# Hybrid decoder layer: the first head's values reloaded in two parts, output weights and residual blocks loaded later

## The chip, the cores and the metric

One Trainium2 chip; the same program runs on 8 of its cores, each on its own 2048 tokens (two sequences of 8192, four cores each), with the 2048 tokens before them as a halo. The metric is the device time of the slowest core in microseconds.

## What is computed

One decoder layer on x (2, 8192, 1024). A parallel mixer, a cross-attention into 256 memory tokens and a SwiGLU network, each behind an RMS norm and added to the residual. The change concerns the attention of the mixer and the loads for what follows it. Cut to that:

```python
proj = rms_norm(x) @ w_in                       # q: 3 groups x 4 heads x 128, k, v: 4 heads x 128, u: 512
for g, (window, dilation) in enumerate(((128, 1), (512, 4), (2048, 16))):
    # query t attends to t - j*dilation, j = 0..window//dilation, shared k and v of head h
    acc[g], m[g], l[g] = dilated_branch(q[:, :, g], k, v, window, dilation)
attn = sum(w[g] * acc[g]) / sum(w[g] * l[g])    # merged over the three groups
h = x + concat([attn, pooled(u)]) @ w_out       # output projection
h = h + cross_attention(rms_norm(h), mem)       # w_cq, w_ckv, w_co
h = h + swiglu(rms_norm(h))                     # d_ff 2816
```

## The kernel before

**Stage 1** walks over 32 tiles of 128 tokens (16 halo, 16 own). For each tile it makes products of the tile of x with the column chunks of w_in (k, v, q0, q1, q2, u). K and Q are kept, transposed, in four slabs of the arena, one per head. V is written tile by tile to a scratch tensor in HBM (`v_scr`, `v_post`), from the ACT queue, since each dilation wants V gathered in another way. Tile 31 comes last, then the u chunks of tiles 28 to 31.

**Attention** has 48 units: `units = (h, r4, g)`, 4 heads, 4 residues of the position modulo 4, and the groups g = 2, 1, 0 (dilation 16, 4, 1). For each unit `S_stage` makes 8, 5 or 17 score matmuls (1024 columns in all) in one of two score tiles in PSUM, ScalarE takes the exponential (128x1024), VectorE multiplies by a mask, and two units later `PV_stage` makes as many numerator matmuls with V and 2 or 3 denominator matmuls with a block of ones. After three units `fin` divides. So three units have 68 matmuls, a head 272.

**V of a head** comes back from HBM in three loads on SP's queue (`load_v`): 1024 KB for dilation 16 (`v16`), 640 KB for dilation 4 (`v4`), 544 KB for dilation 1 (`v1`, runs of 256 bytes). There are two V buffers: V of head h + 2 takes the place of V of head h. The buffer of head 0 lies over the x tiles 20 to 27, that of head 1 over the w_in chunks 2, 3 and 4, of which chunk 2 (u) is read last in stage 1.

**The other loads.** `late_loads`, at unit 1, puts the masks of residues 1 to 3 (768 KB, read as 1.5 MB of float32) on the GpSimd queue, then V of head 1 on SP's, then the output weights `wout` (two loads of 1024 KB) on GpSimd's. The residual blocks xr (2048 KB each, `load_h`) take the place of K and Q slabs that are done with; the memory tokens (`memt`) and the weights w_ckv, w_cq and w_co come at the ends of heads.

**Order.** The program is written once as a list of operations with reads and writes. `order` (line 104) makes each engine's stream of it: it takes, again and again, the operation that can start first by fixed costs, within 160 operations of the oldest open one (40 for a transfer). All transfers go over one modelled bus, so a transfer that is placed early in the program delays the modelled arrival of those behind it, and with it the matmuls that read them. The streams are fixed in the program; on the chip semaphores hold them.

**After attention** `O_units` (output projection of 512 tokens each, added to the residual block), the norms, cross-attention and the feed-forward network are woven together.

Line 306 is every matmul, 309 every transpose, 317 ScalarE's operations, 324, 335 and 339 VectorE's or GpSimd's, 352 a transfer issued by SP, ACT or GpSimd, 355 a load of weights with conversion to bfloat16 on the GpSimd queue.

Of the kernel before, what the change touches and what calls it, by code (L numbers as in the profile page):

```python
# [248 lines left out]
def build_program():  # L249
# [22 lines left out]
    with es:  # L272
# [78 lines left out]
        def DMA(q, out, in_, r, w, **kw):  # L351
            return P.dma(q, lambda e: e.dma_start(out=out, in_=in_, **kw), r, w, nbytes(in_))  # L352
# [36 lines left out]
        def over(keys):  # L389
            return [("~", k) for k in keys]  # L390
# [30 lines left out]
        def load_x(T0, n, r=()):  # L421
            b = T0 // 4
            o = xb[(b + 2) % 3][:, (T0 % 4) * 1024:(T0 % 4 + n) * 1024].rearrange("p (t c) -> p t c", t=n)
            DMA("pool", o, xt_d[T0:T0 + n].rearrange("t p c -> p t c"), list(r),
                [("x", T0 + t) for t in range(n)] + [("~", ("x", T0 + t - 12)) for t in range(n)])
# [215 lines left out]
        for t in range(20, 32):  # L641
# [18 lines left out]
                ("v", 20): [lambda: load_x(24, 4), lambda: WLOAD(mk16, mask_d[:, 0:256], ["mk16"]),  # L660
                            lambda: WLOAD(mk4, mask_d[:, 256:1280], ["mk4"]),
                            lambda: WLOAD(mk1_0, mask_d[:, 1280:2304], [("mk1", 0)])],
                ("v", 24): [lambda: load_x(28, 4)]}
        slot = 0
        seen = set()
        held = {}
        for kind, T in seq:
# [10 lines left out]
            else:  # L678
# [7 lines left out]
                else:  # L686
# [1 line left out]
            run_slot(slot)  # L688
            slot += 1


        VB = [164 * KB, 124 * KB]
        wkeys = lambda cs: [("w", c, kc) for c in cs for kc in range(8)]
        vb_old = [[("x", T) for T in range(20, 28)], wkeys([2, 3, 4])]
        v16 = [view(VB[i], 4096, BF16) for i in range(2)]
        v4 = [view(VB[i] + 8 * KB, 2560, BF16) for i in range(2)]
        v1 = [view(VB[i] + 13 * KB, 17 * 128, BF16) for i in range(2)]
        attnT = view(108 * KB, 4 * 2048, BF16)
        mk1 = [mk1_0] + [view(142 * KB + i * 2 * KB, 1024, BF16) for i in range(3)]
        Pt = [view(156 * KB + i * 2 * KB, 1024, BF16) for i in range(4)]  # L700
        rdt = [view(154 * KB, 512, F32), view(Z + 16 * KB, 512, F32)]
        wout = view(Z, 8192, BF16)
        stage1_small = [("qs", i, j, h) for i in range(3) for j in range(2) for h in range(4)] + [("rt1", i) for i in range(2)] + [("rt2", i) for i in range(2)] + \
                       [("vst", i) for i in range(4)] + [("ust", i) for i in range(3)]

        def load_v(h):
            i = h % 2
            old = [("~", k) for k in vb_old[i]] if h < 2 else []
            vd = v_dram[h]
            allv = [("vd", T) for T in range(32)]  # L710
            DMA("sp", v16[i].rearrange("p (a c) -> p a c", a=2), vd.rearrange("(a p r) d -> p a (r d)", a=2, r=16),
                allv, [("v16", i)] + old)
            DMA("sp", v4[i].rearrange("p (a c) -> p a c", a=5), vd[1536:4096].rearrange("(a p r) d -> p a (r d)", a=5, r=4),
                allv, [("v4", i)] + old)
            DMA("sp", v1[i].rearrange("p (a c) -> p a c", a=17), vd[1920:4096].rearrange("(a p) d -> p a d", a=17),
                allv, [("v1", i)] + old)

        load_v(0)

        def late_loads():  # L720
            WLOAD(view(142 * KB, 3072, BF16), mask_d[:, 2304:5376], [("mk1", i) for i in (1, 2, 3)] + [("~", k) for k in wkeys([4, 5])])
            load_v(1)
            for i in range(2):
                WLOAD(wout[:, i * 4096:(i + 1) * 4096], w_out_d[:, i * 4096:(i + 1) * 4096], [("wout", i)] + [("~", k) for k in stage1_small])

        units = [(h, r4, g) for h in range(4) for r4 in range(4) for g in (2, 1, 0)]
        first_num = set()
# [111 lines left out]
        for u in range(n_u + LAG):  # L839
            run_slot(slot)  # L840
            slot += 1
            if u < n_u:
                S_stage(u)
            v = u - LAG
            if v >= 0:
                PV_stage(v)
                if v % 3 == 2:
                    fin(v // 3)
                h, r4, g = units[v]
                if v == 1:  # L850
                    late_loads()
                if r4 == 3 and g == 0:
                    if h + 2 < 4:
                        load_v(h + 2)
                    if h != 2:
                        load_h(h)
                    if h == 1:
                        DMA("sp", memf, mem_d, (), ["memf"] + over(slabkeys(1)))
                    if h == 2:
                        for i in range(2):  # L860
                            WLOAD(wckv[:, i * 4096:(i + 1) * 4096], w_ckv_d[:, i * 4096:(i + 1) * 4096],
                                  [("wckv", i)] + over(vkeys(0)))
                    if h == 3:
                        WLOAD(wcq, w_cq_d, ["wcq"] + over(slabkeys(3)))
                        WLOAD(wco, w_co_d, ["wco"] + over(slabkeys(3)))
        while pend:
# [242 lines left out]

        weave(O_units(0), (mem_norm_steps(), 0.0, 0.8))  # L1110
        load_h(2)
        weave(O_units(1), (R_steps(0), 0.0, 0.8), (mem_kv_steps(), 0.3, 1.0))
        weave(O_units(2), (R_steps(1), 0.0, 0.8), (Q_steps(0), 0.1, 1.0))
        weave(O_units(3), (R_steps(2), 0.0, 0.8), (X_steps(0), 0.1, 0.9), (Q_steps(1), 0.1, 1.0))
# [216 lines left out]
```

How the kernel before makes its waits and increments, by code:

```python
            def run_stream(e, eh):  # L186
                known = {}
                nw = 0
                for o in self.streams[e]:
                    waits = {}
                    for d in o.deps:
                        key = id(d.sem)
                        if known.get(key, 0) >= d.val:
                            continue
                        if key not in waits or waits[key][1] < d.val:
                            waits[key] = (d.sem, d.val)
                    if o.is_dma and o.prev_val > 0:
                        key = id(o.sem)
                        if known.get(key, 0) < o.prev_val:
                            if key not in waits or waits[key][1] < o.prev_val:
                                waits[key] = (o.sem, o.prev_val)
                    for key, (s, v) in waits.items():
                        eh.wait_ge(s, v)
                        known[key] = v
                        nw += 1
                    ins = o.emit(eh)
                    if o.is_dma:
                        ins.then_inc(o.sem, 16)
                    elif o.needs_inc:
                        ins.then_inc(o.sem, 1)
                if e == "sp":
                    for o in final_wait_ops:
                        if known.get(id(o.sem), 0) < o.val:
                            eh.wait_ge(o.sem, o.val)
                            known[id(o.sem)] = o.val
                stats[e] = (len(self.streams[e]), nw)
```

## Time and profile before

| | us |
|---|---|
| median of 3 runs | 1018.22 (1016.47 to 1074.41) |
| profiled execution, slowest core | 1017.06 |
| its span on core 2, first to last instruction | 1015.5 |
| TensorE busy in it | 957.7 (94%) |
| VectorE, ScalarE, GpSimd busy | 425.3, 385.6, 170.4 |

The page of the profile shows one execution on the slowest core, core 2. The time of the execution is 1.56 us more than this span. Stage 1 ends near 302 us, attention near 390 us; the feed-forward network fills the last half. Busy time of TensorE includes what a slow clock stretches, and a wait is told by its releaser: the semaphore that came last. "issue" is time in which the engine waited for nothing that the profile shows.

### The profile page before, as it was taken

The numbers are of one execution on the slowest core, as the hardware profiler recorded it, in microseconds if no ns is written. First come the engines' busy times: TensorE is split into PE (matmuls) and PEld (weight loads), VectorE is DVE, ScalarE is ACT, GpSimd is POOL, SyncE is SP. The second block draws the span as 40 slices with busy tenths as digits, with TensorE's granted clock in tenths as the row PEclk, the third lists the DMA queues.
The fourth block names the chain that finished last, engine by engine and source line by source line (L and its number), as shares of the span: only waits on it lengthen the run. The fifth ranks groups of instructions, "written<-read, shape, count | busy, mean of one in ns | idle before, by whom it ended". The sixth has DMA issues, their size and how long they took to land.

```text
span 1015.5 us, 16680 instructions; the slowest of 8 cores (1004.2 to 1015.5 us)
## 1 busy us (share of the span) xinstructions
PE 957.7 (94%) x5647; PEld 481.1 (47%) x5752; DVE 425.3 (42%) x934; ACT 385.6 (38%) x726; POOL 170.4 (17%) x253
## 2 busy tenths in 40 slices
PE   2889999999998789999999999999999999999998
PEld 1445545555556675434443444444444444444443
DVE  2436784666764455546677221211133211211111
ACT  3436656555557784446784111111011111111000
POOL 1224452333340011211220000020120000010000
PEclk9989999999998999999999999999999999999999
DMA  9876434110049779300040345547565255538461
GB/s 240 200 126 164 112 53 77 27 38 12 16 107 187 220 211 185 113 0 1 2 84 0 50 76 83 83 76 123 115 115 133 42 83 84 83 60 139 90 133 59
DMA packets 65586, 96.44 MB, mean 95 GB/s; under 512 B 27616, under 2 KB 38752, under 8 KB 63328
## 3 DMA queue, kind: packets, MB, share of 16 engines
q0 software_dynamic: 28496, 50.96, 31.8%
q1 hardware_dynamic: 19968, 40.09, 12.6%
q10 hardware_dynamic: 17040, 4.33, 2.0%
q8 instruction: 48, 0.79, 0.3%
q14 instruction: 34, 0.28, 0.1%
HBM read 133.74 MB, written 12.58 MB: 144 GB/s over the span
## 4 chain that ended last, share of the span: by engine, by line
PE 87%; DMA 4%; issue 2%; ACT 2%; DVE 2%; ACTq 1%; POOL 0%; SPq 0%; DVEq 0%; POOLq 0%
PE psall L306 86%; DMA arena<-v_scr 3%; ACT arena L317 2%; PE psall L309 2%; DMA arena<-xt 1%; DVE arena L335 1%; ACTq L352 1%; DVE arena L324 1%; POOL arena L324 0%; DVE arena L339 0%; DVE arena L329 0%; ACT L317 0%; DVE arena L346 0%; SPq L352 0%; ACTq L203 0%
## 5 line engine op out<-in xcount | busy, mean ns | idle before, releaser
L306 PE MATMUL psall<-arena 128*128 128x512 bf16 (+5 forms) x5327 | 946.0, 335 | 50.9 <-DMA arena<-xt 13.0
L306 PEld LDWEIGHTS psall<-arena 128*128 128x128 bf16 x5432 | 461.0, 100 | 514.4 <-issue 77.6
L317 ACT ACTIVATE arena<-psall 128x512 bf16<-128x512 f32 (+4 forms) x350 | 225.6, 670 | 340.5 <-PE psall L306 316.2
L324 POOL TENSOR_TENSOR arena<-arena 128x256 f32<-128x256 bf16 (+4 forms) x192 | 124.5, 661 | 312.1 <-DVE arena L335 178.0
L324 DVE TENSOR_TENSOR arena<-arena,psall 128x512 bf16<-128x512 f32 x88 | 60.5, 688 | 241.5 <-PE psall L306 232.2
L317 ACT ACTIVATE arena<-arena 128x512 bf16<-128x512 f32 (+6 forms) x292 | 114.2, 410 | 122.2 <-PE psall L306 63.2
L324 DVE TENSOR_TENSOR arena<-psall,arena 128x512 f32<-128x512 f32 (+1 forms) x128 | 86.6, 688 | 172.0 <-PE psall L306 162.5
L335 DVE SCALAR_TENSOR_TENSOR arena<-psall,arena 128x128 bf16<-128x128 f32 (+2 forms) x372 | 111.2, 357 | 61.8 <-ACT arena L317 33.2
L339 DVE TENSOR_REDUCE arena<-arena 128x4 f32<-128x512 bf16 x80 | 54.0, 681 | 50.0 <-ACT arena L317 49.8
L317 ACT ACTIVATE arena<-psall,arena 128x512 bf16<-128x512 f32 (+2 forms) x78 | 52.1, 670 | 39.4 <-PE psall L306 37.3
L355 POOL DMA_DIRECT2D arena<-w_gu_t x22 | 16.6, 753 | 279.1 <-PE psall L306 279.1
L335 DVE SCALAR_TENSOR_TENSOR arena<-arena 128x512 bf16<-128x512 f32 (+2 forms) x75 | 53.5, 750 | 9.5 <-ACT arena L317 8.9
L324 DVE TENSOR_TENSOR arena<-arena 128x1024 bf16<-128x1024 bf16 (+2 forms) x50 | 34.6, 694 | 35.0 <-ACT arena L317 30.2
L309 PEld LDWEIGHTS psall<-arena 128*128 128x128 bf16 x320 | 22.0, 98 | 15.6 <-issue 4.3
L309 PE MATMUL psall<-arena 128*128 128x128 bf16 x320 | 26.5, 219 | 3.1 <-POOL arena L324 3.1
L346 DVE COPY arena<-psall 128x512 bf16<-128x512 bf16 x48 | 24.3, 506 | 11.8 <-PE psall L306 9.7
L317 ACT ACT_TABLE_LOAD x6 | 7.7, 1283 | 47.0 <-PE psall L306 30.2
L355 POOL DMA_DIRECT2D arena<-w_d_t x8 | 7.2, 898 | 108.6 <-PE psall L306 108.6
L355 POOL DMA_DIRECT2D arena<-w_ckv_t x2 | 1.5, 744 | 62.4 <-PE psall L306 62.4
L352 POOL DMA_DIRECT2D arena<-xt x11 | 8.2, 746 | 21.6 <-DMA arena<-xt 19.1
L329 DVE TENSOR_SCALAR arena<-arena 128x512 bf16<-128x512 f32 (+3 forms) x23 | 11.3, 519 | 0.1
L329 POOL TENSOR_SCALAR arena<-arena 128x512 bf16<-128x512 f32 x4 | 6.2, 1561 | 0.0
(14 smaller groups left out, 15.8 us busy)
## 6 DMA issues: line engine op xcount, KB each, us to landing
arena<-w_gu_t POOLq DMA_DIRECT2D x22, 1024.0 KB, 8.6
arena<-w_in_t SPq DMA_DIRECT2D x12, 1024.0 KB, 7.6
arena<-w_d_t POOLq DMA_DIRECT2D x8, 1408.0 KB, 17.5
arena<-xr SPq DMA_DIRECT2D x4, 2048.0 KB, 12.3
outT<-arena SPq DMA_DIRECT2D x32, 256.0 KB, 3.6
arena<-xt POOLq DMA_DIRECT2D x7, 1024.0 KB, 12.3
v_scr<-arena ACTq DMA_DIRECT2D x32, 128.0 KB, 2.7
arena<-v_scr SPq DMA_DIRECT2D x4, 1024.0 KB, 8.1
```

The costliest lines, as they stand in the source:

```text
L306: P.op("pe", lambda e: e.matmul(out, lhsT=lhsT, rhs=rhs, start=start, stop=stop), r, w, max(0.056, 0.003 + size(out) / 2400))
L309: P.op("pe", lambda e: e.transpose(out=out, in_=in_, identity=ident), r, w, 0.057)
L317: P.op("act", lambda e: e.activation(out=out, in_=in_, func=func, **kw), r, w, 0.18 + 0.00085 * size(out))
L324: P.op(eng, lambda e: e.tensor_tensor(out=out, in0=in0, in1=in1, op=op), r, w, dcost(eng, size(out), per))
L329: P.op(eng, lambda e: e.tensor_scalar(out=out, in0=in0, scalar1=s1, scalar2=None, op0=op0), r, w, c)
L335: P.op("dve", lambda e: e.scalar_tensor_tensor(out=out, in0=in0, scalar=scalar, in1=in1, op0=op0, op1=op1, **kw), r, w, dcost("dve", size( ...
L339: P.op("dve", lambda e: e.tensor_reduce(out=out, in_=in_, axis=mybir.AxisListType.X, op=ALU.add), r, w, dcost("dve", size(in_), 0.00105))
L346: P.op(eng, lambda e: e.tensor_copy(out=out, in_=in_), r, w, dcost(eng, size(out), 0.0009))
L352: return P.dma(q, lambda e: e.dma_start(out=out, in_=in_, **kw), r, w, nbytes(in_))
L355: return P.dma("pool", lambda e: e.dma_start(out=out, in_=in_, max_dma_last_dim=4096), r, w, nbytes(in_))
```

## The change

Three things are done.

1. V of head 0 is loaded in two parts. Part 0 is issued at tile 29 of stage 1 and waits for the writes of V of tiles 0 to 27 only: the first half of `v16`, 96 of 128 partitions of its second half, 4 of 5 blocks of `v4`, 13 of 17 of `v1`. Part 1, at the old place, loads the rest (128 KB each) and waits for part 0 and all writes. Heads 1 to 3 are loaded as before.
2. The output weights move from unit 1 to unit 12 (`wout_loads`), and they read the key of the last V load of head 1, so their issue waits until it has landed.
3. The residual blocks 0 and 1 were loaded at the ends of heads 0 and 1; they are now loaded at the ends of heads 2 and 3. Block 3 moves from the end of head 3 to behind block 2, after the first piece of the projection.

```diff
@@ todo of stage 1
-                ("v", 24): [lambda: load_x(28, 4)]}
+                ("v", 24): [lambda: load_x(28, 4)], ("v", 29): [lambda: load_v(0, 0)]}
...
+        def load_v(h, part=None):
+            i = h % 2
+            old = over(vb_old[i]) if h < 2 else []
+            vd = v_dram[h]
+            dep = {0: range(28), 1: range(28, 32), None: range(32)}[part]
+            allv = [("vd", T) for T in dep]
...
+            elif part == 0:
+                DMA("sp", o16[:, 0:1, :], s16[:, 0:1, :], allv, [("v16a", i)] + old)
+                DMA("sp", o16[0:96, 1:2, :], s16[0:96, 1:2, :], allv, [("v16b", i)] + old)
+                DMA("sp", o4[:, 0:4, :], s4[:, 0:4, :], allv, [("v4a", i)] + old)
+                DMA("sp", o1[:, 0:13, :], s1[:, 0:13, :], allv, [("v1a", i)] + old)
+            else:
+                DMA("sp", o16[96:128, 1:2, :], s16[96:128, 1:2, :], allv + [("v16a", i), ("v16b", i)], [("v16", i)] + old)
+                DMA("sp", o4[:, 4:5, :], s4[:, 4:5, :], allv + [("v4a", i)], [("v4", i)] + old)
+                DMA("sp", o1[:, 13:17, :], s1[:, 13:17, :], allv + [("v1a", i)], [("v1", i)] + old)
...
-        load_v(0)
+        load_v(0, 1)
 
         def late_loads():
             WLOAD(view(142 * KB, 3072, BF16), mask_d[:, 2304:5376], [("mk1", i) for i in (1, 2, 3)] + [("~", k) for k in wkeys([4, 5])])
             load_v(1)
+
+        def wout_loads():
             for i in range(2):
-                WLOAD(wout[:, i * 4096:(i + 1) * 4096], w_out_d[:, i * 4096:(i + 1) * 4096], [("wout", i)] + [("~", k) for k in stage1_small])
+                WLOAD(wout[:, i * 4096:(i + 1) * 4096], w_out_d[:, i * 4096:(i + 1) * 4096], [("wout", i)] + over(stage1_small),
+                      r=[("v1", 1)])
@@ the loop over the units
                 if v == 1:
                     late_loads()
+                if v == 12:
+                    wout_loads()
                 if r4 == 3 and g == 0:
                     if h + 2 < 4:
                         load_v(h + 2)
-                    if h != 2:
-                        load_h(h)
                     if h == 1:
                         DMA("sp", memf, mem_d, (), ["memf"] + over(slabkeys(1)))
                     if h == 2:
+                        load_h(0)
...
                     if h == 3:
+                        load_h(1)
                         WLOAD(wcq, w_cq_d, ["wcq"] + over(slabkeys(3)))
...
         weave(O_units(0), (mem_norm_steps(), 0.0, 0.8))
         load_h(2)
+        load_h(3)
```

The stream of SP from the last w_in chunks on, before (`v_scr` rows are V loads: 128x2x2048 is dilation 16, 128x5x512 dilation 4, 128x17x128 dilation 1; xr is a residual block):

```order
L352 DMA arena<-w_in_t 128x2048 x4
L352 DMA arena<-v_scr 128x2x2048
L352 DMA arena<-v_scr 128x5x512
L352 DMA arena<-v_scr 128x17x128
L352 DMA arena<-v_scr 128x2x2048
L352 DMA arena<-v_scr 128x5x512
L352 DMA arena<-v_scr 128x17x128
L352 DMA arena<-v_scr 128x2x2048
L352 DMA arena<-v_scr 128x5x512
L352 DMA arena<-xr 128x4096
L352 DMA arena<-v_scr 128x17x128
```

The same place of SP now, up to the last V load of head 1:

```order
L352 DMA arena<-w_in_t 128x2048 x4
L352 DMA arena<-v_scr 128x2048
L352 DMA arena<-v_scr 96x2048
L352 DMA arena<-v_scr 128x4x512
L352 DMA arena<-v_scr 128x13x128
L352 DMA arena<-v_scr 32x2048
L352 DMA arena<-v_scr 128x512
L352 DMA arena<-v_scr 128x4x128
L352 DMA arena<-v_scr 128x2x2048
L352 DMA arena<-v_scr 128x5x512
L352 DMA arena<-v_scr 128x17x128
```

Seven smaller loads of head 0 stand for three. The residual block that stood inside V of head 2 is gone from there; all four blocks now follow the last V load of head 3.

The stream of TensorE in head 2 before, from the denominators of its first three units on (128x4x16 x15 with 128x4x8 x2 are the seventeen numerators of dilation 1, 128x8x4x16 to 128x2x4x8 its denominators, 128x64 x15 with 128x32 x2 its scores, 128x128 x8 scores or numerators of dilation 16):

```order
L306 MATMUL psall<-arena 128x8x4x16
L306 MATMUL psall<-arena 128x7x4x16
L306 MATMUL psall<-arena 128x2x4x8
L306 MATMUL psall<-arena 128x128 x8
L306 MATMUL psall<-arena 128x4x16 x15
L306 MATMUL psall<-arena 128x4x8 x2
L306 MATMUL psall<-arena 128x4x16 x15
L306 MATMUL psall<-arena 128x4x8 x2
L306 MATMUL psall<-arena 128x64 x15
L306 MATMUL psall<-arena 128x32 x2
L306 MATMUL psall<-arena 128x64 x4
```

And now, in the same head:

```order
L306 MATMUL psall<-arena 128x4x16 x15
L306 MATMUL psall<-arena 128x4x8 x2
L306 MATMUL psall<-arena 128x8x4x16
L306 MATMUL psall<-arena 128x7x4x16
L306 MATMUL psall<-arena 128x2x4x8
L306 MATMUL psall<-arena 128x64 x15
L306 MATMUL psall<-arena 128x32 x2
L306 MATMUL psall<-arena 128x128 x8
```

Before, the numerators of two units of dilation 1 stood in one run, behind the denominators of both; the same happened in head 3. Now each unit's numerators stand ahead of its denominators throughout head 2, and in head 3 the numerators of one unit alone come late, between two denominator matmuls of the unit behind it. The stream of GpSimd is the same row for row: the output weights were and are its next transfers behind the masks, and only what they wait for is new.

## Rows read from the trace of the kernel before

**Rows 1.** Cores: span and mean granted TensorE clock.
```profile
core 1: 1012.5 us, clock 0.997
core 2: 1015.5 us, clock 0.992
...
core 4: 1004.2 us, clock 0.998
...
core 6: 1013.9 us, clock 0.993
```

**Rows 2.** Chain that ended last, core 2: start us, length us, what.
```profile
302.13 32.95 DMA arena<-v_scr
```

**Rows 3.** Timeline of TensorE, core 2: start us, length us, group [idle before <-releaser].
```profile
305.62 8.42 PE L306 MATMUL psall<-arena 128*128 128x64 bf16 x130 [0.51 <-ACT arena L317]
317.38 11.00 PE L306 MATMUL psall<-arena 128*128 128x64 bf16 x134 [3.34 <-DVE arena L324]
328.53 4.25 PE L306 MATMUL psall<-arena 128*128 128x64 bf16 x67 [0.15 <-DVE arena L324]
335.33 5.44 PE L306 MATMUL psall<-arena 128*128 128x64 bf16 x87 [2.55 <-DMA arena<-v_scr]
343.32 8.99 PE L306 MATMUL psall<-arena 128*128 128x64 bf16 x114 [2.56 <-issue]
```

**Rows 4.** Waits, core 2, 295 to 400 us: total us, times, longest us.
```profile
DVE arena L324 <- DMA arena<-masks: 4.5, 1, 4.5
...
PE psall L306 <- issue: 2.6, 1, 2.6
PE psall L306 <- DMA arena<-v_scr: 2.5, 1, 2.5
```

**Rows 5.** Windows, core 2: length, busy (x), then PEclk, DMA share, GB/s.
```profile
315.00:320.00 5.00, 2.62 (x39) 2.15 (x40) 2.49 (x4) 0.81 (x2) 0.00 (x0) 0.64 1.05 175
320.00:325.00 5.00, 4.95 (x52) 3.97 (x51) 2.08 (x3) 3.13 (x4) 0.00 (x0) 0.68 1.05 167
...
340.00:345.00 5.00, 2.44 (x41) 2.02 (x38) 1.83 (x3) 2.73 (x4) 0.00 (x0) 0.87 0.82 254
345.00:350.00 5.00, 4.95 (x68) 4.10 (x68) 1.88 (x3) 2.82 (x5) 0.00 (x0) 0.79 0.14 36
```

**Rows 6.** DMA, core 2, 302 to 320 us; issues with KB and us to landing.
```profile
q0 software_dynamic: 732, 1.47, 54.5%
q1 hardware_dynamic: 1170, 1.76, 39.8%
...
arena<-v_scr SPq DMA_DIRECT2D x1, 544.0 KB, 33.0
```

**Rows 7.** DMA, core 2, the V loads of head 0: issue, then us to landing.
```profile
288.78 1.47 SPq L352 DMA_DIRECT2D arena<-v_scr  x3
...
arena<-v_scr SPq DMA_DIRECT2D x1, 544.0 KB, 10.5
```

**Rows 8.** Timeline of GpSimd, core 2: issue of the output weights.
```profile
309.32 1.52 POOL L355 DMA_DIRECT2D arena<-w_out_t  x2 [7.59 <-PE psall L306]
```

**Rows 9.** Windows, core 4: length, busy (matmuls first), PEclk, DMA share, GB/s.
```profile
315.40:344.60 29.20, 26.11 (x410) 21.63 (x417) 16.60 (x24) 24.52 (x31) 0.00 (x0) 1.00 0.87 219
344.80:373.50 28.70, 24.42 (x390) 20.32 (x396) 16.31 (x24) 23.92 (x31) 3.20 (x4) 1.00 0.89 242
```

**Rows 10.** Timeline of TensorE, core 4.
```profile
333.67 2.46 PE L306 MATMUL psall<-arena 128*128 128x64 bf16 x40 [2.24 <-issue]
```

**Rows 11.** Timeline of SP's queue, core 2.
```profile
328.57 2.48 SPq L352 DMA_DIRECT2D arena<-xr  x1
331.57 20.32 SPq L352 DMA_DIRECT2D arena<-v_scr  x3
...
388.72 18.03 SPq L352 DMA_DIRECT2D arena<-xr  x2
```

**Rows 12.** Waits of TensorE, 295 to 420 us: core 1, then core 6.
```profile
PE psall L306 <- DMA arena<-v_scr: 1.0, 1, 1.0
...
PE psall L306 <- DMA arena<-v_scr: 3.1, 1, 3.1
```

More of the change, by code:

```diff
@@ L662, in build_program @@
                             lambda: WLOAD(mk1_0, mask_d[:, 1280:2304], [("mk1", 0)])],
-                ("v", 24): [lambda: load_x(28, 4)]}
+                ("v", 24): [lambda: load_x(28, 4)], ("v", 29): [lambda: load_v(0, 0)]}
+        VB = [164 * KB, 124 * KB]
+        wkeys = lambda cs: [("w", c, kc) for c in cs for kc in range(8)]
+        vb_old = [[("x", T) for T in range(20, 28)], wkeys([2, 3, 4])]
+        v16 = [view(VB[i], 4096, BF16) for i in range(2)]
+        v4 = [view(VB[i] + 8 * KB, 2560, BF16) for i in range(2)]
@@ new lines, in build_program @@
+        v1 = [view(VB[i] + 13 * KB, 17 * 128, BF16) for i in range(2)]
+        attnT = view(108 * KB, 4 * 2048, BF16)
+        mk1 = [mk1_0] + [view(142 * KB + i * 2 * KB, 1024, BF16) for i in range(3)]
+        Pt = [view(156 * KB + i * 2 * KB, 1024, BF16) for i in range(4)]
+        rdt = [view(154 * KB, 512, F32), view(Z + 16 * KB, 512, F32)]
+        wout = view(Z, 8192, BF16)
+        stage1_small = [("qs", i, j, h) for i in range(3) for j in range(2) for h in range(4)] + [("rt1", i) for i in range(2)] + [("rt2", i) for i in range(2)] + \
+                       [("vst", i) for i in range(4)] + [("ust", i) for i in range(3)]
@@ new lines, in load_v @@
+        def load_v(h, part=None):
[4 more added lines that the diff above has]
+            allv = [("vd", T) for T in dep]
+            o16 = v16[i].rearrange("p (a c) -> p a c", a=2)
+            s16 = vd.rearrange("(a p r) d -> p a (r d)", a=2, r=16)
+            o4, s4 = v4[i].rearrange("p (a c) -> p a c", a=5), vd[1536:4096].rearrange("(a p r) d -> p a (r d)", a=5, r=4)
+            o1, s1 = v1[i].rearrange("p (a c) -> p a c", a=17), vd[1920:4096].rearrange("(a p) d -> p a d", a=17)
+            if part is None:
+                DMA("sp", o16, s16, allv, [("v16", i)] + old)
+                DMA("sp", o4, s4, allv, [("v4", i)] + old)
+                DMA("sp", o1, s1, allv, [("v1", i)] + old)
+            elif part == 0:
[7 more added lines that the diff above has]
+                DMA("sp", o1[:, 13:17, :], s1[:, 13:17, :], allv + [("v1a", i)], [("v1", i)] + old)
@@ L689, in build_program @@
             slot += 1
[L692 to L716, printed above, removed]
-        load_v(0)
+        load_v(0, 1)
         def late_loads():
```

## The prediction

> **What bounds the kernel now.** I read the spans of the cores first [rows 1]. The job ends with its slowest core: core 2 needs 1015.5 us, core 4, which does the same work, 1004.2 us. So some 11 us of core 2's span are waits, not work. Then the chain that ended last: it is TensorE nearly throughout, and its longest piece that isn't is a transfer of the values V into the arena, from 302 to 335 us [rows 2]. That is where attention begins. The timeline of TensorE there [rows 3] shows three stops on core 2: 3.34 us before 317.38, 2.55 us before 335.33, 2.56 us before 343.32. The waits of that stretch [rows 4] name the first two. VectorE waited for the masks (4.5 us) and TensorE for VectorE; then TensorE waited for V. The third has no releaser, only "issue". The windows [rows 5] show what a stop costs on top: after the first the granted clock is 0.64 and 0.68 for 10 us, after the last 0.87 and 0.79 (a mix of full 2.4 GHz and 1.2 GHz).
>
> The reader is to see who fills the DMA engines in that stretch. From 302 to 320 us the GpSimd queue (masks, then output weights) takes 54.5% of the sixteen engines, SP's queue (V of head 1) 39.8%; together they are full. The last V transfer of head 1, 544 KB, takes 33.0 us to land [rows 6]. The same 544 KB of head 0, with no such company, took 10.5 us [rows 7].
>
> **The split load of head 0.** Before, its three loads are issued from 288.78 us on and have landed by about 300.4 [rows 7]. TensorE comes to the first products with V only in the stretch that begins at 305.62 us, and the one wait for V in these waits is the later one of 2.55 us [rows 3, 4]. So there is nothing to gain on this path: 0. It adds four DMA issues on SP, which has nothing else to do then, some 1.9 MB of reading while the last four tiles of stage 1 run, and 0.4 MB behind the last write of V. I count 0 to 1 us of cost. The Trainium skill (DMA: Bandwidth & Descriptors, Rules for kernel authors) says of two transfers to disjoint partition halves that they serialise and aren't worth it. By that rule this part is a small loss of fixed costs; the row gives it no wait to shorten either, so both leave the sum as it is.
>
> **The output weights, off the path of V of head 1.** They were issued at 309.32 us [rows 8]; now they wait until the last V load of head 1 has landed. In rows 6 the GpSimd queue spends 54.5% of 18 us, 9.8 us of all engines, on 1.47 MB, or 6.7 us per MB; SP's spends 7.2 us on 1.76 MB, or 4.1 us per MB. Masks (0.79 MB) then cost 5.2 us, V of a head (2.26 MB) 9.3 us, the weights (2.1 MB) 14 us. The transfers start near 303.4 us, so masks and V of head 1 are done by 318, say 320 with the landing. TensorE wants the last of them at 328.53 + 4.25 = 332.8 us [rows 3]. The wait of 2.55 us goes. The next thing late there is VectorE or ScalarE by a few tenths. With it goes most of the half-speed window: 0.13 and 0.21 of 5 us each are 1.7 us of lost clock [rows 5]; I take 1.5, bounds 0 and 1.7.
>
> **The order of heads 2 and 3.** The stream of each engine comes from a list scheduler that charges every transfer to one bus. With the early residual block and weights gone, it moves matmuls: before, in heads 2 and 3, the seventeen numerators of two groups stood in a row and three score tiles bunched behind them; now the pattern of heads 0 and 1 goes on through head 2, and in head 3 one group is displaced by a little. What the bunching costs stands in the windows of core 4 [rows 9]. From 315.40 to 344.60 us 410 matmuls take 29.20 us with one stop of 2.24 [rows 10], so 26.96 / 410 = 65.8 ns each; from 344.80 to 373.50 us 390 take 28.70, or 73.6 ns, with no stop like it. A head has 272, so two heads lose 2 x 272 x 7.8 ns = 4.2 us. Since a piece of disorder stays in head 3, I take 4.0, bounds 0 and 4.2. This is paid on every core.
>
> **The residual blocks.** The block of 2 MB issued at 328.57 us among V of head 2, and the next one, now stand behind all V loads [rows 11]. They are needed when the projection begins, about 389 us, where the last two blocks are released by the end of the last scores; from 350 us on they have over 30 us. Two blocks of 2.1 MB at 4.1 us per MB take 17 us of all engines. Cover: heads 2 and 3. Cost 0; the queue of SP has nothing behind them that is due.
>
> **The stop marked "issue".** Its length differs by core: 2.56 us on core 2, 2.24 on core 4 [rows 3, 10]. Since no semaphore releases it, I read it as code that comes late because the DMA engines are full. They are full in after too, but without the big residual block. I take 1.5 us left, so 1.0 gained; bounds 2.6 gained and 2.6 lost (a second one in the new full stretch). The Trainium skill (Runtime: NRT & Kernel Launch, Instruction fetch mechanics) calls the cost of crossing a block of instructions mostly hidden. By it this term would be 0; the trace disagrees if my reading of the stop is right.
>
> **What stays.** The masks keep their place and their trigger, so I leave the stop of 3.34 us and its slow window.
>
> Sum for core 2: 2.55 + 1.5 + 4.0 + 1.0 = 9.05, so 1015.5 - 9.05 = 1006.4 us. Core 1 (1012.5 us, V wait 1.0 us [rows 12]) gives 1012.5 - 1.0 - 4.0 - 1.0 = 1006.5; core 6 (1013.9 us, V wait 3.1) gives 1013.9 - 3.1 - 1.5 - 4.0 = 1005.3. The slowest of eight is a little above such estimates: 1007. The profiled execution took 1017.06 us, 1.56 us more than its span, hence 1008.6 us. That execution lies 1.2 us below the median of 1018.22, so a median for the changed kernel is near 1009; I forecast 1009.0.
>
> **Rivals.** (1) The weights starve V of head 2: slower. They now run from about 320 us, and V of head 2 is issued in the ten microseconds after, its last part by 331.57 us [rows 11]. The regular order also wants its last part much sooner: one head after 332.8, that is 332.8 + 272 x 65.8 ns = 350.7 us. By my bus count all is done by 320 + 14 + 9.3 = 343 to 345 us. But if the 544 KB need 33.0 us again, as beside the weights in rows 6, they land at 364.6, TensorE stops for 14 us, and a slow window costs 2 us more (between the 1.7 and 3.4 of rows 5): 1008.6 + 16 = 1024.6 us. It decides from a landing time of 350.7 - 331.6 = 19 us on. For it: that row. Against it: those 33 us also held the masks and the residual block, and the weights here have a lead of some 6 us. The Trainium skill (DMA: Bandwidth & Descriptors, Queues, rings and completion order) has each engine take turns between the queues packet by packet; a late V load would then lose half its rate to the weights for as long as they last, which is the mechanism of this rival, and in rows 6 the two queues do share about evenly.
> (2) The gain is smaller: the stop marked "issue" comes back elsewhere and a longer one is added, and the regular order gives half since ScalarE is nearly full anyway. 1015.5 - 2.55 - 1.5 - 2.0 + 2.6 = 1012.0, so 1013.6 us. For it: the DMA engines stay full from 303 to past 345 us.
> (3) The masks land sooner too, because the weights of neighbouring cores no longer run: core 2 gains 3.34 us and up to 3.4 us of clock more [rows 5], but then core 1 sets the end at about 1006, so 1007 us at most and 1004 if "issue" stops shrink too. Against it: the masks are issued before the weights, in the same queue.
>
> **How the numbers follow.** Forecast 0.55, (1) 0.12, (2) 0.23, (3) 0.10. The range for 8 in 10 goes from (3) to beyond (2): 1003 to 1018 us. Faster or slower by over 2% (about what a measurement of this kernel can tell from no change) means below 998 or above 1038.6 us; no case reaches either, which leaves 0.03 and 0.02 for the unforeseen.
>
> **What would show it.** Right: no wait of TensorE for V; the 544 KB of head 1 landed by about 320 us; core 4 at 66 ns per matmul in the stretch of heads 2 and 3; the stop for the masks still there on core 2. Wrong: a stop before the last numerators of head 2's first group (rival 1), new "issue" stops past 340 us (rival 2), masks landing within 12 us on core 2 (rival 3), or a later end of stage 1, moved by the early reads of V.

## The result and the profile after

| | before | after |
|---|---|---|
| median of 5 runs, us | 1018.22 (1016.47 to 1074.41) | 1028.7 (1026.89 to 1157.35) |
| profiled execution | 1017.06 | 1028.79 |
| its span | 1015.5 (core 2) | 1026.9 (core 0) |
| first residual addition of the output projection to the end | 622.2 | 641.4 |

The ratio is 1.0104, 95% interval 1.0086 to 1.0121: slower, by 10.5 us, where 9 us less were forecast. In some executions the cores of one die ran at a lower clock throughout: the medians of this table count them, while the ratio and every time given below leave them out.

In the two profiled executions every core is slower (core 5 by 3.1 us, core 4 by 19.0), so this is in the program, not in one core's luck. The windows of core 0 tell where (length, then busy time and count of TensorE's matmuls, its weight loads, VectorE, ScalarE and GpSimd; then PEclk, DMA share, GB/s):

```profile
300.00:395.00 95.00, 83.81 (x1190) 64.70 (x1205) 50.46 (x75) 74.30 (x100) 12.03 (x16) 1.00 0.91 212
395.00:430.00 35.00, 29.94 (x146) 14.54 (x147) 16.97 (x28) 10.61 (x22) 5.56 (x5) 0.95 0.38 96
430.00:465.00 35.00, 25.76 (x90) 9.54 (x90) 11.67 (x18) 10.93 (x17) 3.12 (x3) 0.76 0.00 0
465.00:1027.00 562.00, 553.85 (x2515) 249.95 (x2565) 162.74 (x239) 130.03 (x208) 46.33 (x52) 1.00 0.43 77
```

The two middle stretches on core 2 of before, begun 7.8 us later since its first residual addition is at 393.29 us and that of after at 385.50:

```profile
402.80:437.80 35.00, 33.96 (x171) 16.31 (x173) 17.64 (x29) 13.64 (x27) 6.45 (x6) 1.00 0.38 97
437.80:472.80 35.00, 33.55 (x150) 14.20 (x152) 20.02 (x30) 18.78 (x30) 6.60 (x6) 1.00 0.00 1
```

From 430 to 465 us TensorE does 90 matmuls where it did 150, its granted clock is 0.76, and no DMA engine is busy. So it isn't a transfer that is waited for. Attention, ahead of it, runs at full clock and better than before. The waits of TensorE show both. First 300 to 395 us of after, core 0 (total us, times, longest), which answers to rows 4 and 12:

```profile
PE psall L306 <- issue: 3.3, 3, 1.9
PE psall L306 <- ACT arena L317: 3.1, 5, 1.2
PE psall L306 <- DVE arena L324: 3.1, 4, 2.5
```

No wait for V is left, on any core. Now 395 to 470 us of after:

```profile
PE psall L306 <- DVE arena L335: 9.0, 5, 3.2
PE psall L306 <- ACT arena L317: 2.6, 4, 1.1
PE psall L306 <- DVE arena L324: 2.4, 1, 2.4
PE psall L306 <- issue: 0.2, 1, 0.2
```

and 387 to 465 us of before, core 2:

```profile
PE psall L306 <- ACT arena L317: 1.3, 4, 0.5
PE psall L306 <- DVE arena L335: 0.8, 1, 0.8
```

That is 14.2 us of stops in place of 2.1. The timeline of TensorE and then of VectorE there (start us, length us, group, [idle before <-releaser]) tells what VectorE was doing:

```profile
439.25 0.38 PE L306 MATMUL psall<-arena 128*128 128x512 bf16 x1 [0.41 <-ACT arena L317]
442.84 2.72 PE L306 MATMUL psall<-arena 128*128 128x512 bf16 x6 [3.21 <-DVE arena L335]
...
447.25 0.58 PE L306 MATMUL psall<-arena 128*128 128x512 bf16 x1 [0.84 <-ACT arena L317]
450.45 3.57 PE L306 MATMUL psall<-arena 128*128 128x512 bf16 x8 [2.62 <-DVE arena L335]
```

```profile
437.30 4.73 DVE L335 SCALAR_TENSOR_TENSOR arena<-arena 128x512 bf16<-128x512 f32 x7 [0.92 <-ACT arena L317]
441.94 0.75 DVE L335 SCALAR_TENSOR_TENSOR arena<-psall,arena 128x512 bf16<-128x512 f32 x1
...
449.55 0.75 DVE L335 SCALAR_TENSOR_TENSOR arena<-psall,arena 128x512 bf16<-128x512 f32 x1 [6.20 <-ACT arena L317]
```

Two kinds of work share line 335, and the operands tell them apart: `arena<-arena` scales a token block by its norm (`rms_steps`), `arena<-psall,arena` scales a query of cross-attention out of PSUM (`norm_tail`), which TensorE's next product reads. Seven of the first kind stand in a row, 4.73 us, and the one for which TensorE waits stands behind them; TensorE has nothing else in its stream at that point and stops for 3.21 us. Later VectorE itself is idle for 6.20 us behind ScalarE, while TensorE runs single matmuls between stops.

VectorE was no quicker at that place in before. Its rows and TensorE's there, core 2:

```profile
438.32 2.74 DVE L335 SCALAR_TENSOR_TENSOR arena<-arena 128x512 bf16<-128x512 f32 x4 [0.92 <-ACT arena L317]
...
442.84 0.75 DVE L335 SCALAR_TENSOR_TENSOR arena<-psall,arena 128x512 bf16<-128x512 f32 x1
```

```profile
441.19 8.34 PE L306 MATMUL psall<-arena 128*128 128x512 bf16 x37 [0.54 <-ACT arena L317]
```

From the start of the row of scalings to the scaling of the query it is 4.52 us in before and 4.64 us after. The difference is that TensorE then ran 37 matmuls in one piece across that scaling, where it now has a single one (at 439.25) and stops. So these rows put the loss in cover that TensorE's stream has lost, not in more work on VectorE. Behind the stops the granted clock is lower: where it was 1.00 it is now 0.95 and 0.76.

The sizes agree: 12.1 us more of stops, and by an estimate from the windows 29.94 x 0.05 + 25.76 x 0.24 = 7.7 us of the busy time lost to the clock, together 19.8 us; the table above has 641.4 - 622.2 = 19.2 us. The end of stage 1 moved little: the group of 25 matmuls that follows its last transposes starts at 304.30 us, before at 303.41. Attention gave its part: from there to the first residual addition it is 81.2 us, before 89.9. The time is lost behind that point and nowhere else.

### The profile page after: what moved, and what is told of

Same layout as the page of the kernel before. It is cut to its first block, busy times and chain, and to the rows that moved or that the text cites. A ratio compares the mean times of both kernels' runs of the same rounds, so it can differ in the third digit from the quotient of the medians.

```text
span 1026.9 us, 16716 instructions; the slowest of 8 cores (1015.6 to 1026.9 us)
## 1 busy us (share of the span) xinstructions
PE 960.3 (94%) x5647; PEld 479.9 (47%) x5752; DVE 425.8 (41%) x934; ACT 385.6 (38%) x726; POOL 170.1 (17%) x253
## 4 chain that ended last, share of the span: by engine, by line
PE 86%; DVE 4%; issue 3%; DMA 3%; ACT 2%; ACTq 1%; POOL 0%; DVEq 0%; POOLq 0%
PE psall L306 85%; ACT arena L317 2%; DVE arena L335 2%; DMA arena<-masks 1%; PE psall L309 1%; DMA arena<-xt 1%; DVE arena L324 1%; ACTq L352 1%; DVE arena L339 1%; DVE arena L329 0%; POOL arena L324 0%; DVE arena L346 0%; ACT L317 0%; DVEq L203 0%; ACTq L203 0%
## 5 line engine op out<-in xcount | busy, mean ns | idle before, releaser
L306 PE MATMUL psall<-arena 128*128 128x512 bf16 (+4 forms) x5327 | 948.5, 335 | 59.6 <-DVE arena L335 15.9
L306 PEld LDWEIGHTS psall<-arena 128*128 128x128 bf16 x5432 | 459.6, 100 | 526.9 <-issue 91.4
L317 ACT ACTIVATE arena<-psall 128x512 bf16<-128x512 f32 (+4 forms) x350 | 226.1, 670 | 333.9 <-PE psall L306 310.6
L324 POOL TENSOR_TENSOR arena<-arena 128x256 f32<-128x256 bf16 (+4 forms) x192 | 124.3, 661 | 331.1 <-DVE arena L335 168.2
L317 ACT ACTIVATE arena<-arena 128x512 bf16<-128x512 f32 (+5 forms) x292 | 113.4, 409 | 137.2 <-PE psall L306 66.8
L324 DVE TENSOR_TENSOR arena<-arena,psall 128x512 bf16<-128x512 f32 x88 | 60.6, 688 | 241.4 <-PE psall L306 235.2
L324 DVE TENSOR_TENSOR arena<-psall,arena 128x512 f32<-128x512 f32 (+1 forms) x128 | 86.7, 688 | 172.7 <-PE psall L306 166.6
L335 DVE SCALAR_TENSOR_TENSOR arena<-psall,arena 128x128 bf16<-128x128 f32 (+2 forms) x372 | 111.2, 357 | 83.8 <-ACT arena L317 48.6
L339 DVE TENSOR_REDUCE arena<-arena 128x4 f32<-128x512 bf16 x80 | 54.0, 681 | 49.2 <-ACT arena L317 49.1
L317 ACT ACTIVATE arena<-psall,arena 128x512 bf16<-128x512 f32 (+2 forms) x78 | 52.1, 671 | 41.4 <-PE psall L306 38.6
L335 DVE SCALAR_TENSOR_TENSOR arena<-arena 128x512 bf16<-128x512 f32 (+2 forms) x75 | 53.0, 747 | 7.4 <-ACT arena L317 6.9
L324 DVE TENSOR_TENSOR arena<-arena 128x1024 bf16<-128x1024 bf16 (+2 forms) x50 | 34.6, 694 | 25.9 <-ACT arena L317 22.2
L309 PEld LDWEIGHTS psall<-arena 128*128 128x128 bf16 x320 | 22.2, 98 | 15.8 <-issue 4.5
L346 DVE COPY arena<-psall 128x512 bf16<-128x512 bf16 x48 | 24.3, 505 | 12.0 <-PE psall L306 9.7
(14 smaller groups left out, 15.8 us busy)
```

Of the source, the lines that this page charges most:

```text
L306: P.op("pe", lambda e: e.matmul(out, lhsT=lhsT, rhs=rhs, start=start, stop=stop), r, w, max(0.056, 0.003 + size(out) / 2400))
L309: P.op("pe", lambda e: e.transpose(out=out, in_=in_, identity=ident), r, w, 0.057)
L317: P.op("act", lambda e: e.activation(out=out, in_=in_, func=func, **kw), r, w, 0.18 + 0.00085 * size(out))
L324: P.op(eng, lambda e: e.tensor_tensor(out=out, in0=in0, in1=in1, op=op), r, w, dcost(eng, size(out), per))
L335: P.op("dve", lambda e: e.scalar_tensor_tensor(out=out, in0=in0, scalar=scalar, in1=in1, op0=op0, op1=op1, **kw), r, w, dcost("dve", size( ...
L339: P.op("dve", lambda e: e.tensor_reduce(out=out, in_=in_, axis=mybir.AxisListType.X, op=ALU.add), r, w, dcost("dve", size(in_), 0.00105))
```

## Experiments

Three theories. **O**: the loss is the order of the streams behind attention, which the scheduler makes otherwise because the residual blocks now stand on its one modelled bus ahead of the later weights. **T**: the transfers themselves, late or crowded. **S**: the split loads cost in stage 1. The order of TensorE's, ScalarE's and VectorE's computing instructions was read from the built programs, which is why the expectations can speak of it. Before was run beside every kernel; its medians were 1016.83 us (beside e1 to e4), 1016.66 (e5 to e8) and 1017.30 (e9 to e12). The ratio is an estimate of its own from the same executions, so it can differ by 0.001 from the quotient of two medians.

### The first four: parts alone, and order against transfers

**e1**, the residual blocks back:

```diff
                 if h + 2 < 4:
                     load_v(h + 2)
+                if h != 2:
+                    load_h(h)
...
-                    load_h(0)
...
-                    load_h(1)
...
         load_h(2)
-        load_h(3)
```

> The changed kernel with the residual blocks loaded where they were before (blocks 0, 1 and 3 behind the loads of V at the ends of heads 0, 1 and 3), the split V and the late output weights kept. The order of every engine's instructions behind attention is then that of the kernel before. Theory O (the loss is the order of the engines' instructions behind attention, which the residual blocks' new place has changed): the stretch from the first output projection to the end goes back from 646 to about 627 us, the gains at the start of attention stay; 1008 to 1012 us. Theory T (late arrivals or crowding by the late output weights): 1018 us or more. Theory S (the split loads cost in stage 1): 1018 us or more, with stage 1 longer.

Measured 1015.78 us, ratio 0.9987 (0.9974 to 1.0). The loss is gone, as O has it: on core 7 it is 622.3 us from the first residual addition (390.59) to the end. The gain is nearly gone too, which O did not say, so the time misses the 1008 to 1012 us expected. The waits of core 7, 300 to 400 us, show why:

```profile
PE psall L306 <- ACT arena L317: 5.8, 9, 1.2
PE psall L306 <- DMA arena<-v_scr: 3.4, 1, 3.4
```

ScalarE's many short stops are those of before, since the old place of the blocks brings a bunched order of heads 2 and 3 with it; and there is a wait for V again, now at 351 us for head 2, whose last load stands behind residual block 0 on SP's queue and beside the output weights. It is the place that the first rival named, but that rival blamed the weights alone and had 16 us; here it is 3.4 us, and e12 will show that it takes the block.

**e2**, of the whole change the split alone:

```diff
         def late_loads():
...
             load_v(1)
-
-        def wout_loads():
             for i in range(2):
...
-                if v == 12:
-                    wout_loads()
```

(together with e1's diff; the output weights are loaded at unit 1 again and wait for no load of V)

> The kernel before with the split V of head 0 alone; output weights and residual blocks where they were. Theory O: no order of an engine's computing instructions changes, only SP's; the wait for V (2.55 us and a part of the 1.5 us of clock) may go or may stay, as the output weights still stand before it: 1014 to 1018.5 us. Theory S: 1020 us or more.

Measured 1017.01 us, ratio 0.9993 (0.9977 to 1.0008). S is out. The split by itself does nothing that these executions can tell from no change.

**e3**, the changed kernel with before's order behind attention. A table names, for each engine, the stretches of its stream and the operations in them by their number in the program; transfers stay where they are:

```diff
+FIXED = {
+    "pe": [(2992, [(4271, 3), (4267, 1), (4274, 5), (4280, 12),
...
+}
...
+        comp = [o for o in self.ops if not o.is_dma]
+        for e, parts in FIXED.items():
+            st = self.streams[e]
+            at = [i for i, o in enumerate(st) if not o.is_dma]
+            for first, runs in parts:
+                new = [comp[k] for a, n in runs for k in range(a, a + n)]
...
+                for j, o in enumerate(new):
+                    st[at[first + j]] = o
```

> All transfers as in the changed kernel, but a table puts the instructions of TensorE, ScalarE and VectorE behind attention in the order that they have in the kernel before. Theory O: the 18 us of the stretch behind attention come back, 1008 to 1012 us, TensorE's stops of 2 to 3.5 us between 404 and 455 us gone and its clock at 1.00 there. Theory T (the transfers themselves, the residual blocks or weights that land late): 1025 to 1030 us, since every transfer is issued as in the changed kernel.

Of four executions two count, 1009.87 and 1011.57 us (median 1010.72), too few for a ratio. The 18 us are back, with every transfer issued as in the changed kernel: T is out. Windows and waits of the profiled execution, core 5 (the table makes the file longer, so each line has a number higher by 15: L321 is L306, L332 is L317, L339 is L324 and L350 is L335); the waits are those of 387 to 470 us:

```profile
387.00:430.00 43.00, 42.16 (x213) 20.14 (x212) 22.35 (x36) 15.91 (x31) 8.52 (x8) 1.00 0.46 112
430.00:465.00 35.00, 33.59 (x152) 14.05 (x151) 20.32 (x30) 18.60 (x30) 6.70 (x6) 1.00 0.00 1
```

```profile
PE psall L321 <- ACT arena L332: 1.4, 4, 0.5
PE psall L321 <- DVE arena L350: 0.8, 1, 0.8
PE psall L321 <- DVE arena L339: 0.2, 1, 0.2
```

The clock is 1.00 throughout; 2.4 us of stops stand where 14.2 stood. From the first residual addition (385.00 us) to the end of the span (1008.3) it is 623.3 us, where before has 622.2.

**e4**, the converse: the same table code in the kernel before, with the changed kernel's order behind attention.

> All transfers as in the kernel before, but TensorE, ScalarE and VectorE have the changed kernel's order behind attention. Theory O: the loss without the gains, 18 us more than before, 1033 to 1038 us. Theory T: 1016 to 1020 us, as before.

Measured 1035.01 us, ratio 1.0168 (1.0144 to 1.0191), 17 to 18 us over before. The waits of core 2, 390 to 470 us, are those of the changed kernel within 0.3 us, the window shows the clock, and from the first residual addition (392.88) to the end it is 640.9 us:

```profile
PE psall L321 <- DVE arena L350: 9.0, 5, 3.2
PE psall L321 <- DVE arena L339: 2.4, 1, 2.4
PE psall L321 <- ACT arena L332: 2.3, 4, 0.8
```

```profile
430.00:465.00 35.00, 26.06 (x94) 9.97 (x95) 11.45 (x17) 12.12 (x19) 3.12 (x3) 0.83 0.00 1
```

O stands on both legs: the order alone makes the loss, and without it the loss isn't there.

### The next four: what the gain consists of, and a remedy

**e5**, as e3, but the table holds before's order for attention as well.

> All transfers as in the changed kernel, but every engine's computing instructions in the order of the kernel before, in attention too. It differs from e3 only in the order of heads 2 and 3. By the prediction's sum that order is worth 4.0 us of the 7 or so that e3 gained (ScalarE's ten short stops of TensorE, 5.6 us in all, come back for 1.9): 1012 to 1015 us. If the transfers alone made the gain: 1008 to 1011 us. If the order made all of it: 1016 to 1018 us.

Measured 1012.27 us, ratio 0.9947 (0.9929 to 0.9965), as the prediction's sum would have it. So the new transfers alone give 4.4 us by the medians (1016.66 - 1012.27) and 5.4 by the ratio, whose interval allows 3.6 to 7.2. The order of heads 2 and 3 gives some 1.5 on top of it (1012.27 to 1010.72), but with two executions of e3 that can't be told from nothing.

**e6**, the remedy that O suggests. The scheduler's model takes the residual blocks at no cost; on the chip they are transferred as in the changed kernel:

```diff
         def DMA(q, out, in_, r, w, **kw):
-            return P.dma(q, lambda e: e.dma_start(out=out, in_=in_, **kw), r, w, nbytes(in_))
+            return P.dma(q, lambda e: e.dma_start(out=out, in_=in_, **kw), r, w, 0 if w and w[0][0] == "hT" else nbytes(in_))
```

> The changed kernel in which the scheduler's model of the one bus takes the four residual blocks at no cost; nothing else is edited. Attention's order stays the changed kernel's; behind attention the order becomes neither kernel's, nearer that of before. Theory O with the cause in the modelled bus: the loss goes, 1007 to 1013 us. If another order than that of before is as bad as the changed kernel's: 1020 us or more.

Measured 1005.81 us, ratio 0.9884 (0.9841 to 0.9927): with one edit of the model the changed kernel is 23 us faster than it was, and 11 us faster than before by the medians (12 by the ratio). Its four executions (1004.79 to 1008.2 us) also lie under e3's two, so before's order behind attention wasn't the best either. Waits of core 1, 387 to 470 us:

```profile
PE psall L306 <- ACT arena L317: 0.3, 1, 0.3
PE psall L306 <- DVE arena L335: 0.2, 1, 0.2
PE psall L306 <- DVE arena L324: 0.2, 1, 0.2
```

0.7 us of stops, where before had 2.1 and after 14.2. From the first residual addition (384.95) to the end (1005.0) it is 620.1 us, 2.1 under before; the other 8.3 us of the gain lie ahead of it.

**e7**, e6 with the masks in three transfers:

```diff
-            WLOAD(view(142 * KB, 3072, BF16), mask_d[:, 2304:5376], [("mk1", i) for i in (1, 2, 3)] + [("~", k) for k in wkeys([4, 5])])
+            for i in (1, 2, 3):
+                WLOAD(mk1[i], mask_d[:, 1280 + 1024 * i:2304 + 1024 * i], [("mk1", i)] + [("~", k) for k in wkeys([4, 5])])
```

> As e6, and the masks of the late tiles loaded in three transfers of 256 KB in place of one of 768 KB. The stop of TensorE for the masks (2 to 3.3 us on some cores) goes or shrinks: 1 to 4 us under e6. Rival: the two issues more on POOL and the other transfers put back by them cost as much, within 1 us of e6.

Measured 1008.65 us, ratio 0.9906 (0.9869 to 0.9943): 2.8 us over e6 by the medians, outside both expectations. The stop did go: TensorE's longest wait for VectorE between 300 and 387 us is 0.6 us over all eight cores, where e6 has 3.1. But the stops marked "issue" rose from 2.5 to 3.7 us a core (table below). The intervals overlap, so whether it is slower than e6 stays open; a gain of 1 us or more isn't seen.

**e8**, e3 with `load_v(0)` whole again, behind the last tile:

```diff
-                ("v", 24): [lambda: load_x(28, 4)], ("v", 29): [lambda: load_v(0, 0)]}
+                ("v", 24): [lambda: load_x(28, 4)]}
...
-        load_v(0, 1)
+        load_v(0)
```

> As e3, with the values of the first head loaded in one part again, behind the last tile: what the split is worth where the output weights are out of the way. If the split hides the wait: 2 to 4 us more than e3, 1011 to 1014 us, with TensorE waiting 1 to 3 us for V at about 302. If the late output weights alone took that wait away: as e3, 1009 to 1011 us.

Measured 1009.43 us, ratio 0.992 (0.9889 to 0.9951), and no wait for V on any core. The split is worth nothing that can be seen; the late output weights took the wait away.

### The last four: the remedy taken apart

**e9**, the kernel before with the table for attention alone, so that heads 2 and 3 run in the changed kernel's order.

> All transfers as in the kernel before, and behind attention its order too; heads 2 and 3 alone in the changed kernel's order. e3 against e5 gives this order 2 us with the changed kernel's transfers. If it is worth as much with the transfers of before: 1014 to 1016.5 us, ScalarE's ten stops at four. If its gain needs V and the weights in the new order: 1016.5 to 1019 us.

Measured 1014.86 us, ratio 0.9977 (0.9964 to 0.999), 2.4 us under before. Its timeline of TensorE on core 3 shows what takes a part of the gain away:

```profile
336.96 13.21 PE L321 MATMUL psall<-arena 128*128 128x64 bf16 x181 [5.49 <-DMA arena<-v_scr]
```

A wait for V of 5.49 us, where before's cores had 3.1 at most: without the later weights the same load is late.

**e10**, e6's edit in the kernel before, nothing else.

> The kernel before with one edit: the model takes the residual blocks at no cost. Every transfer is issued where it was before; the order behind attention becomes that of e6, and that of attention all but the changed kernel's. If e6's 1005.8 us rests on the order alone: 1005 to 1009 us. If order and transfers each give their part (2 to 5 us for the order of both stretches, 5.7 us for the transfers by e5): 1011 to 1015 us.

Measured 1012.47 us, ratio 0.995 (0.9933 to 0.9968): 4.8 us by orders alone (5.1 by the ratio). Order and transfers each give a part.

**e11**, e6 and e8's diff together: the values in one part, the blocks free in the model.

> As e6, with the values of the first head in one part behind the last tile. e8 against e3 says that the split gives nothing once the output weights are out of the way: 1004 to 1007.5 us. If e3's 1010 us hid a gain of the split: 1008 us or more.

Measured 1007.54 us, ratio 0.9902 (0.9879 to 0.9924). At the expected bound; it is 1.7 us over e6 by the medians, but the intervals overlap.

**e12**, e11 with e1's diff: residual blocks at their old places.

> As e11, with the residual blocks loaded where they were before (ends of heads 0, 1 and 3): block 0 of 2 MB goes ahead of head 2's values, beside the output weights. The order of the computing instructions is that of e6 and e11. If e1's wait for V at 351 us (3.4 us) comes from that block: the wait shows again, 1009 to 1013 us. If the place of the residual blocks doesn't matter to the transfers: 1004 to 1007.5 us.

Measured 1008.80 us, ratio 0.9911 (0.9887 to 0.9935). TensorE on core 7 waits for V of head 2, and the load that it waits for took 24.3 us, where the changed kernel's two loads of that size on core 0 in its stretch from 320 to 350 us took 15.0 in the median:

```profile
353.52 17.32 PE L306 MATMUL psall<-arena 128*128 128x64 bf16 x272 [2.48 <-DMA arena<-v_scr]
```

```profile
arena<-v_scr SPq DMA_DIRECT2D x1, 544.0 KB, 24.3
```

```profile
arena<-v_scr SPq DMA_DIRECT2D x2, 544.0 KB, 15.0
```

The wait that was expected is there, and e11, which has the same weights but not the block at that place, has it on no core. It reaches three of eight cores and costs 1.3 us of the median, within the noise of the two intervals.

All kernels side by side: stops of TensorE between 300 and 387 us, mean over the eight cores of one execution, worked out from the waits of each core (longest single one in brackets); clock as the mean of the cores' windows.

| | V | ScalarE | VectorE | issue | clock 300-387 | clock 387-465 | us |
|---|---|---|---|---|---|---|---|
| before | 1.4 (3.1) | 5.5 | 1.7 (3.3) | 3.4 (3.1) | 0.972 | 0.998 | 1017.3 |
| after | 0 | 1.9 | 1.4 (2.5) | 3.3 (2.4) | 0.990 | 0.883 | 1028.4 |
| e1 | 1.1 (3.4) | 5.5 | 1.1 (2.0) | 2.7 (2.8) | 0.990 | 1.000 | 1015.8 |
| e2 | 0.8 (3.3) | 5.5 | 1.5 (3.1) | 6.0 (8.4) | 0.960 | 1.000 | 1017.0 |
| e3 | 0 | 1.9 | 1.2 (2.5) | 3.1 (2.3) | 0.995 | 1.000 | 1010.7 |
| e4 | 1.6 (4.5) | 5.6 | 1.6 (3.0) | 1.9 (3.1) | 0.985 | 0.895 | 1035.0 |
| e5 | 0 | 5.4 | 0.5 (1.3) | 3.0 (2.8) | 0.995 | 1.000 | 1012.3 |
| e6 | 0 | 1.6 | 1.4 (3.1) | 2.5 (2.3) | 0.992 | 1.000 | 1005.8 |
| e7 | 0.1 (0.5) | 1.8 | 1.1 (0.6) | 3.7 (2.1) | 0.998 | 1.000 | 1008.7 |
| e8 | 0 | 1.9 | 1.0 (1.2) | 3.9 (2.8) | 0.988 | 1.000 | 1009.4 |
| e9 | 2.9 (5.5) | 1.9 | 1.7 (3.2) | 2.2 (2.8) | 0.972 | 1.000 | 1014.9 |
| e10 | 0.3 (1.5) | 1.9 | 2.2 (3.7) | 7.3 (8.8) | 0.953 | 1.000 | 1012.5 |
| e11 | 0 | 2.0 | 1.1 (2.0) | 3.9 (2.8) | 0.990 | 1.000 | 1007.5 |
| e12 | 0.7 (2.5) | 1.9 | 1.8 (2.7) | 3.1 (2.8) | 0.990 | 1.000 | 1008.8 |

(Before's 1017.3 is its median beside e9 to e12.)

## Why the prediction was wrong

The direction was wrong, and one step made it so. The term by term account, in the prediction's own order:

- **Split load, cost 0.** Right as far as the noise allows: e2 has 0.9993, and e8 and e11, without it, can't be told from e3 and e6, which have it.
- **Output weights, 2.55 + 1.5 us.** Right in mechanism, near in size. No core waits for V; the last V load of head 1 lands in 15.8 us after its issue in place of 33.0 [rows 6]; the clock of the stretch rose from 0.972 to 0.990, 1.6 us of 87 (a mean over cores). The weights, which wait for that load, are issued at 320.48 us on core 0, so V had landed by about 320 us, as the sign asked. e5, which holds the orders fixed, gives all transfers together 5.4 us by its ratio where the terms 2.55, 1.5 and 1.0 make 5.05. The load that lands in after, in the DMA view of 302 to 320 us:

```profile
arena<-v_scr SPq DMA_DIRECT2D x1, 544.0 KB, 15.8
```

- **Order of heads 2 and 3, 4.0 us.** The work per matmul fell as said. Core 4 of after, which answers to rows 9, has one unbroken group:

```profile
336.74 37.57 PE L306 MATMUL psall<-arena 128*128 128x64 bf16 x587 [0.63 <-issue]
```

  37.57 / 587 = 64.0 ns, where 65.8 was expected and before had 73.6. ScalarE's stops fell by 3.6 us a core (5.5 to 1.9). Of the time of the kernel it made less: 2.4 us in e9, where the wait for V grew, and about 1.5 from e5 to e3. So 4.0 was about twice too much.
- **"issue", 1.0 us gained.** Wrong: 3.3 us a core against 3.4, and 3.9 in e8 and e11.
- **Masks stay, with their slow window.** Half right. The stop is there on some cores (2.51 us on core 0 of after, 2.38 on core 4) but gone on core 2, which the sign named: there the masks land in 11.2 us in place of 15.5, the sign of rival 3. Cores 0, 4 and 6 still need 14.6 to 14.8 us, and in before cores 4 and 7 had 11.3 already, so rival 3 as a whole did not occur; which core is late changes, and a sign tied to one core says little. The slow window doesn't always follow: the clock from 315 to 320 us is 1.00 on core 0 of after, 0.66 on core 4.
- **Residual blocks, "Cost 0; the queue of SP has nothing behind them that is due".** This is the step that failed. It priced the blocks as transfers on the chip, where they do cost nothing that can be seen (T is out). But they are also entries on the scheduler's modelled bus. The prediction knew that bus and used it for heads 2 and 3, and stopped looking there. At the ends of heads 2 and 3 stand the weights for cross-attention; each block of 2.1 MB ahead of them takes 10 us of a bus modelled at 210 KB per us, so the model thinks the weights late and orders everything behind attention for that. The cost in place of 0 was 17 to 18 us (e4, and e3 against after): e4 shows it without the moved transfers, e6 takes it away with the modelled price of the blocks alone. e6 frees all four blocks at once, so which of them does it isn't shown.
- **Rival 1**, V of head 2 starved by the weights, did not occur: no core of after waits for V. e1 and e12 show a wait at that place, of 3.4 and 2.5 us at most, where block 0 stands ahead of the last of those loads. So moving the blocks helped the queue, by about 1 us, and hurt in the model.
- **The last step of the sum.** 1008.6 us and the 1.2 us by which that execution lay under the median make 1009.8; the text rounds this down to 1009.0. It changes nothing here.

The attention's part of the forecast came out near in size: 7.8 us earlier at the first residual addition, 8.7 from the end of stage 1 on, against 9.05 forecast. In part that is luck. From 300 to 387 us the stops of TensorE fall by 5.0 us between core 2 of before and core 0 of after (14.5 to 9.5), and the clock goes from 0.94 to 1.00, by an estimate 4.3 us of 71.43 busy ones, where the sum has 1.5; that makes up for the order's missing half and for "issue". What was missing is a look at all places at which the new streams differ from the old. The comparison of orders would have shown that TensorE's, ScalarE's and VectorE's streams differ in a second stretch, behind attention, where the trace of before has only 2.1 us of stops, so that a new order could gain about as much (e6 and e10 did) and could lose far more. What is not settled: which of the moved operations there does the harm: the stream of one engine can't be exchanged without the others, since they would wait for each other in a circle, and smaller exchanges weren't tried.

## What to carry to other kernels

Where a scheduler works from modelled costs, a moved transfer is priced twice: on the chip, and in the model, where it can reorder engines far behind the place of the edit. List every stretch in which the streams differ and ask of each how much the trace of before leaves to gain there; one with 2 us of stops can gain 2 us and lose many times that. And when parts of a change help and the whole does not, hold the order fixed and change the transfers, then the other way round: two runs (e3, e4) settled here what undoing the change part by part (e1) only blurred.

## What was not expected of the hardware

The stops marked "issue" can be much longer than before's trace shows. In e10 (core 0) TensorE stood for 6.50 us with no semaphore to wait for, and 8.8 us is the longest on any core; e2 has 8.4. The timeline of TensorE, and the DMA queues from 309 to 323 us (packets, MB, share of sixteen engines):

```profile
322.20 1.72 PE L306 MATMUL psall<-arena 128*128 128x128 bf16 x11 [6.50 <-issue]
```

```profile
q0 software_dynamic: 851, 1.68, 71.5%
q1 hardware_dynamic: 2594, 0.95, 27.1%
q8 instruction: 1, 0.02, 0.4%
q14 instruction: 2, 0.02, 0.3%
```

The two queues fill the engines to 98.6%, and three instruction packets have to pass between them. Where the weights wait for V of head 1 (after, e1, e3, e5 to e8, e11, e12) no stop of this kind exceeds 2.8 us; where they don't wait, two of five kernels (e2, e10) show one over 8 us and three (before, e4, e9) none over 3.1. That the stops are instructions fetched late fits, but no run isolates it. The Trainium skill (Runtime: NRT & Kernel Launch, Instruction fetch mechanics) calls the cost of crossing from one block of instructions to the next mostly hidden; these rows show stretches in which it isn't, if that reading holds.

The clock followed the stops without any transfer beside them: 0.76 on core 0 of after from 430 to 465 us at a DMA share of 0.00, and 1.00 on e3 in the same window with the same transfers. Whoever prices a group of stops of 2 to 3 us should add what the clock takes, here by the estimate above 7.7 us on 12.1 us of stops. For a single stop these traces give no fixed price: from 315 to 320 us the clock is 1.00 on core 0 of after beside a stop of 2.51 us, and 0.66 on core 4 behind one of 2.38.
